# Seven block products for six gate pairs, with weight sums made by accumulating transfers and tiles turned through memory

## The reference

```
h = rms_norm(x); proj = h @ w_in            # 2048 x 24576: q, k, v, z / u, b, c, z / q, k, v, z, three gates
o_a = dilated_mixture_attn(q, k, v) * silu(z)
o_c = b * causal_short_conv(c * u) * silu(z)
o_r = retention(rotary(q), rotary(k), v) * silu(z)
merged = sum over the three mixers of sigmoid(gate) * (o @ w_branch)     # 1536 -> 2048 each
x = x + rms_norm(merged @ w_out)
```

## Time and profile before

| | us |
|---|---|
| median of 3 runs (2746.15 to 2746.77) | 2746.62 |
| span of the profiled execution | 2743.0 |
| PE busy (share of the span) | 2732.6 (100%) |
| DVE busy | 1924.2 (70%) |
| ACT busy | 1222.0 (45%) |
| DMA, queue of SP, share of the 16 engines | 57.4% |

### The profile page before, as it was taken

One profiled execution on the slowest core, in us unless ns is written; L12 is line 12 of the kernel. 1 busy time (PEld: TensorE's weight loads), 2 busy tenths in 40 slices (PEclk: granted clock), 3 DMA queues, 4 the chain that ended last, 5 costly groups with the idle time before them and its releaser, 6 DMA issues.

```text
span 2743.0 us, 30433 instructions
## 1 busy us (share of the span) xinstructions
PE 2732.6 (100%) x12264; PEld 2268.3 (83%) x12264; DVE 1924.2 (70%) x2558; ACT 1222.0 (45%) x1404; POOL 27.5 (1%) x35
## 2 busy tenths in 40 slices
PE   9999999999999999999999999999999999999998
PEld 7888888888888888888878888888888888888887
DVE  6788744777655898858567887457676558977584
ACT  6454544444443334444454545444444433434443
POOL 0000000000000000000000000000000000000000
PEclk9999999999999999999999999999999999999999
DMA  9555566565555555556575555555656565555563
GB/s 333 184 172 196 170 200 194 190 199 188 196 195 190 184 184 176 182 195 221 180 238 175 184 190 179 197 188 187 202 193 198 188 197 177 191 171 182 199 215 138
DMA packets 264732, 529.10 MB, mean 193 GB/s; under 512 B 8464, under 2 KB 8848, under 8 KB 264336
## 3 DMA queue, kind: packets, MB, share of 16 engines
q1 hardware_dynamic: 260976, 517.50, 57.4%
q10 hardware_dynamic: 2608, 4.78, 0.5%
q0 software_dynamic: 1008, 4.87, 0.5%
HBM read 522.94 MB, written 4.19 MB: 192 GB/s over the span
## 4 chain that ended last, share of the span: by engine, by line
PE 99%; DVE 0%; issue 0%; ACT 0%; DVEq 0%; POOL 0%; POOLq 0%
PE ps L651 32%; PE ps L652 32%; PE ps L653 32%; PE ps L586 0%; PE ps L606 0%; PE ps L604 0%; PE ps L603 0%; PE ps L582 0%; PE ps L567 0%; PE ps L587 0%; PE ps L581 0%; PE ps L669 0%; DVE gates L1183 0%; DVE w_trail L913 0%; DVEq L231 0%
## 5 line engine op out<-in xcount | busy, mean ns | idle before, releaser
L913 DVE TENSOR_TENSOR w_trail<-raw,w_lead 128x1024 fp32r<-128x1024 f32 x973 | 1188.7, 1225 | 763.8 <-ACT w_lead L723 754.4
L723 ACT ACTIVATE w_lead<-raw 128x1024 fp32r<-128x1024 f32 x973 | 1028.3, 1060 | 1394.1 <-PE ps L653 1387.3
L651 PE MATMUL ps<-w_lead,hT_lead 128*128 128x512 f32 x3328 | 1299.1, 390 | 0.8 <-issue 0.4
L653 PE MATMUL ps<-w_lead,hT_trail 128*128 128x512 f32 x3328 | 1295.2, 389 | 0.0
L652 PE MATMUL ps<-w_trail,hT_lead 128*128 128x512 f32 x3328 | 1295.1, 389 | 0.0
L651 PEld LDWEIGHTS ps<-w_lead,hT_lead 128*128 128x128 f32 x3328 | 625.0, 188 | 131.1 <-issue 2.2
L653 PEld LDWEIGHTS ps<-w_lead,hT_trail 128*128 128x128 f32 x3328 | 624.9, 188 | 130.0
L652 PEld LDWEIGHTS ps<-w_trail,hT_lead 128*128 128x128 f32 x3328 | 625.1, 188 | 128.4
L651 PE MATMUL ps<-w_lead,oT_lead 128*128 128x512 f32 x576 | 224.3, 389 | 0.0
L653 PE MATMUL ps<-w_lead,oT_trail 128*128 128x512 f32 x576 | 224.1, 389 | 0.0
L652 PE MATMUL ps<-w_trail,oT_lead 128*128 128x512 f32 x576 | 224.1, 389 | 0.0
(11 more groups left out here) (102 smaller groups left out, 781.7 us busy)
## 6 DMA issues: line engine op xcount, KB each, us to landing
raw<-w_in SPq DMA_DIRECT2D x381, 1024.0 KB, 5.1
raw<-w_out SPq DMA_DIRECT2D x32, 1024.0 KB, 5.0
raw<-w_branch_a SPq DMA_DIRECT2D x24, 1024.0 KB, 5.0
raw<-w_branch_c SPq DMA_DIRECT2D x24, 1024.0 KB, 5.0
raw<-w_branch_r SPq DMA_DIRECT2D x24, 1024.0 KB, 5.0
raw<-w_in SPq DMA_DIRECT2D x5, 512.0 KB, 5.0
gates<-x SPq DMA_DIRECT2D x4, 512.0 KB, 13.5
post_gain<-post_norm_g POOLq DMA_DIRECT2D x2, 1024.0 KB, 8.2
```

The costliest lines, as they stand in the source:

```text
L651: pe.matmul(acc, lead[:, k, tok(t)], wl, start=(k == 0), stop=False)
L653: last = pe.matmul(acc, trail[:, k, tok(t)], wl, start=False, stop=(k == BLOCKS[n][2] - 1))
L723: act.activation(w_lead[:, h % SPLIT_SLOTS, :], raw[:, i % RAW_SLOTS, part:part + HALF * COLS], ACT.Copy).then_inc(lead_ready, 1)
L913: dve.tensor_tensor(w_trail[:, s, :], raw[:, i % RAW_SLOTS, part:part + HALF * COLS], w_lead[:, s, :].bitcast(F32), ALU.subtract).then_inc ...
```

## The change

**Seven products.** Gate blocks 2 and 3 of each mixer (three pairs in a layer, six in all) are computed together for contraction tiles 0 to 7. The activations there are four blocks (two token tiles by two chunks), the weights four blocks (two chunks by two gate blocks); eight block products become seven, on sums of blocks. A product takes one chunk and one 128-token operand: two units of 6 matmuls. Contraction tiles 8 to 15 of both blocks stay as they were (eight units of 12). `PAIR_ORDER` gives the order: p1, q3, two plain units, q5, two plain units, p2, p6, p7, two plain, q4, two plain. p1, p6 and p7 accumulate in one side bank, which ACT copies out after each of them; q5 has another.

**Weight sums.** q5, p6 and q4 take the chunk of p1 with a further chunk added to it each time, p7 takes that of q3. POOL issues each addition as a DMA from memory with `accum_op=ADD` into the raw slot, once the chunk's former form has been split: 4 of 1 MB for a pair, 24 in all. The sums of activations are made once a layer, at units 16 to 19 (`form_work` on DVE, `form_lead_of` on ACT).

**Tiles through memory.** q, k, z and the conv product are written to a scratch tensor in memory (512 KB, one DMA on the queue of ACT) and read back as four DMAs of 128 KB that place the 32-row bands; ACT waits for the write before it issues the reads. DVE then turns the tile in 2 instructions of 128x512 in place of 16. For this the evictions write columns in another order, and PE reads the weights of the blocks other than v in runs of 32 columns (`columns`).

**Beside it**: five raw slots, a slot plan (`raw_slots`), the cos and sin tables widened (constants 128x1968 in place of 128x1328), `post_gain` in the v and q tiles, a negated `x_rstd` from POOL.

```diff
-RAW_SLOTS = 4
+RAW_SLOTS = 5
+PAIRED_GATES = {"attention": (2,), "conv": (2,), "retention": (2,)}
+PRODUCTS = {"p1": ((0, 0), None), "q5": ((0, 0), (1, 0)), "p6": ((0, 0), (1, 1)), "p7": ((1, 1), (1, 0)),
+            "q3": ((1, 1), None), "p2": ((0, 1), None), "q4": ((0, 0), (0, 1))}
+PAIR_ORDER = ("p1", "q3", 0, 0, "q5", 0, 0, "p2", "p6", "p7", 1, 1, "q4", 1, 1)
+SUM_AFTER = {"q5": "p1", "p7": "q3", "p6": "q5", "q4": "p6"}
+PAIR_COPY_DUE = {UNIT_AT[kind, n, 1] + AHEAD: (kind, n) for n in PAIRS for kind in ("p1", "p6", "p7")}
+PAIR_REST_DUE = {UNIT_AT[kind, n, 1] + AHEAD + 1: (kind, n) for n in PAIRS for kind in ("p6", "p7")}
+SUM_DUE = {UNIT_AT[before, n, 1]: (kind, n) for n in PAIRS for kind, before in SUM_AFTER.items()}
...
 ACT_DUE = due({
-    "attention": [("exp", 4 * B + 1), ("out", 6 * B + 1)],
+    "attention": [("q_away", 2 * B - 1), ("q_back", 2 * B + 1), ("k_away", 3 * B - 1), ("k_back", 3 * B + 1),
+                  ("exp", 4 * B + 1), ("z_away", 5 * B + 4), ("z_back", 5 * B + 6), ("out", 6 * B + 1)],
...
# SP, a chunk's load
-                    sp.wait_ge(trail_ready, l * HALVES + (2 * i + 2) + (l == 0 and i == RAW_SLOTS))
+                    slot, _before, free_at = SLOT_OF[l, i]
+                    if free_at is not None:
+                        sp.wait_ge(*split_done(*free_at))
...
# POOL
+            def chunk_sum(l, what, n):
+                (i, c), (added, row) = PRODUCTS[what]
+                slot = SLOT_OF[l, CHUNK_LIST.index((n + i, c))][0]
+                wait(*split_done(l, UNIT_AT[SUM_AFTER[what], n, CHUNK // HALF - 1]))
+                pool.dma_start(raw[:, slot, :].rearrange("p (k n) -> p k n", k=CHUNK),
+                               weights[name][:, at:at + CHUNK, col:col + COLS],
+                               accum_op=ALU.add).then_inc(summed[SUMMED_FOR[what]], 16)
...
+                rstd(x_sum, x_mean, l + 1, x_rstd, D_MODEL, 2).then_inc(x_pow, 1)
+                pool.wait_ge(x_pow, l + 1)
+                pool.tensor_scalar(x_neg, x_rstd, -1.0, 0.0, ALU.mult, ALU.add).then_inc(x_rstd_ready, 1)
...
# PE
+            def product(l, h, what, n, part):
+                if part == 0:
+                    if what == "q5":
+                        pe.wait_ge(*side_bank_free(l, q_step))
+                        pe.wait_ge(form_trail, TILES * (l + 1))
+                    elif what in ("p6", "p7"):
+                        pe.wait_ge(pair_copied, 2 * pair_no(l, n) + 1 + (what == "p7"))
+                    elif what == "q3":
+                        pe.wait_ge(*bank_free(l, n + 1))
+                pe.wait_ge(*split_done(l, h))
...
+                for i in range(HALF):
...
+                    pe.matmul(acc[:, :], lead, wl, start=opens, stop=False, skip_group_check=again)
+                    pe.matmul(acc[:, :], lead, wt, start=False, stop=False, skip_group_check=again)
+                    last = pe.matmul(acc[:, :], trail, wl, start=False, stop=closes, skip_group_check=again)
...
+            def columns(n, ap):
+                if kind == "mix" and role != "v":
+                    return ap.rearrange("p (h j a) -> p j h a", h=HPB, j=QUADS)
-                    wl = w_lead[:, slot, i * COLS:(i + 1) * COLS]
+                    wl = columns(n, w_lead[:, slot, i * COLS:(i + 1) * COLS])
...
# ACT
+                elif what in SUM_AFTER and part == 0:
+                    act.wait_ge(*sum_landed(l, what, n))
...
+            def pair_copy(l, what, n):
+                act.wait_ge(*done_product(l, what, n))
+                copied = act.activation(dst, side(l, step)[:, :], ACT.Copy)
...
+            def send_away(l, what, mixer, g):
+                act.dma_start(bounce[to], tile.rearrange("p t c -> p (t c)")).then_inc(away[to], 16)
+            def bring_back(l, what, mixer, g):
+                act.wait_ge(away[to], 16 * trips(l, to, mixer, g))
+                rows = bounce[to].rearrange("(i b) (j c) -> j b i c", i=QUADS, j=QUADS)
+                for j in range(QUADS):
+                    act.dma_start(tile[SQ * j:SQ * (j + 1), :].rearrange("b (i c) -> b i c", i=QUADS),
+                                  rows[j]).then_inc(back[to], 16)
...
+                elif kind == "gate" and n in PAIR_OF:
+                    act.wait_ge(*moved_out(l, n))
+                        act.activation(gates[:, t, cols], gates[:, t, cols], ACT.Sigmoid,
+                                       scale=x_rstd[:, t:t + 1]).then_inc(gate_ready, 1)
...
# DVE
+            def pair_rest_of(l, what, n):
+                rest = dve.tensor_tensor(gates[:, t, COLS * (j + 1):COLS * (j + 2)], side(l, q_step)[:, :],
+                                         gates[:, t, COLS * col:COLS * (col + 1)], ALU.subtract)
...
+            def form_work(l, what):
...
+            def turn_back(l, what, mixer, g):
+                dve.wait_ge(back[to], 16 * QUADS * trips(l, to, mixer, g))
+                for t in range(TILES):
+                    last = dve.transpose(dst[:, :, tok(t)].rearrange("p h (i b) -> p h i b", i=QUADS), squares[:, t])
```

More of the change, by code:

```diff
@@ L75, in layer_blocks @@
                                ("mix", mixer, role, g)))
-        for j in range(OUT_BLOCKS):
-            blocks.append(("w_in", COLS * (GATES_AT + OUT_BLOCKS * b + j), KT, ("gate", mixer, "", j)))
-        for j in range(OUT_BLOCKS):
-            blocks.append((mixer, COLS * j, KT_MIX, ("branch", mixer, "", j)))
+        for kind, j in TAIL[mixer]:
+            if kind == "gate":
+                blocks.append(("w_in", COLS * (GATES_AT + OUT_BLOCKS * b + j), KT, ("gate", mixer, "", j)))
+            else:
+                blocks.append((mixer, COLS * j, KT_MIX, ("branch", mixer, "", j)))
     for j in range(OUT_BLOCKS):
@@ L165, with unit_after @@
 TURNS = ((0, 3), (3, 6), (6, 9), (9, 12), (12, 14), (14, 16))
+STARTS = [0]
+for _kind, _n, _at in UNITS:
+    STARTS.append(STARTS[-1] + (1 if _kind in PRODUCTS else TILES))
+def unit_after(n, at):
+    return next(h for h in range(HALVES) if STARTS[h] >= STARTS[FIRST_HALF[n]] + TILES * at)
 def due(table, offset=0):
@@ new lines @@
+DVE_DUE = due({
+    "attention": [("q", 2 * B + 4), ("k", 3 * B + 4), ("scores", 4 * B), ("sums", 4 * B + 2)]
+                 + pieces("probs", 4 * B + 3) + [("values", 5 * B + 3), ("z", 6 * B), ("out", 6 * B + 2)],
+    "conv": [("prod", 2 * B + 6), ("conv0", 2 * B + 6), ("conv1", 2 * B + 7), ("conv2", 3 * B),
+             ("gate", 4 * B), ("z", 4 * B + 6), ("product", 4 * B + 6), ("out", 4 * B + 7)],
+    "retention": [("q", 2 * B + 6), ("k", 3 * B + 5), ("scores", 3 * B + 7), ("values", 4 * B + 3),
+                  ("norm", 4 * B + 4), ("gate", 4 * B + 5), ("z", 5 * B + 2), ("out", 5 * B + 4)]}, AHEAD)
@@ L215, with side_list @@
 MERGE_TRAIL_DUE = {h + 1: j for h, j in MERGE_LEAD_DUE.items()}
-RESIDUAL_DUE = FIRST_HALF[MERGE_BLOCK0 + OUT_BLOCKS] + AHEAD + 1
+RESIDUAL_DUE = FIRST_HALF[BLOCK_NO["out", "", "", 0]] + AHEAD + 1
+def side_list():
+    steps = [("x", t, j) for t, j in X_ORDER]
+    for h, (kind, n, at) in enumerate(UNITS):
+        if kind in ("p1", "q5") and at == 0:
+            steps.append(("pair", kind, n))
+        for what, mixer, g in PE_DUE.get(h, []):
+            steps += [(what, mixer, g, i) for i in range(HPB if what == "scores" else HPB // 2)]
+        if h in MERGE_DUE:
+            steps += [("merge", MERGE_DUE[h], t) for t in range(TILES)]
+    return steps
+SIDE_LIST = side_list()
+SIDE_STEPS = len(SIDE_LIST)
+STEP = {key: m for m, key in enumerate(SIDE_LIST)}
+READY_STEPS = [sum(key[0] != "pair" for key in SIDE_LIST[:m]) for m in range(SIDE_STEPS + 1)]
+FORMS = {"p6": 0, "q3": 1, "p7": 2, "q5": 3}
+FORM_STEPS = ("whole", "sums", "lead", "trail")
+FORMS_FROM = 2 * B
+PAIR_COPY_DUE = {UNIT_AT[kind, n, 1] + AHEAD: (kind, n) for n in PAIRS for kind in ("p1", "p6", "p7")}
+PAIR_REST_DUE = {UNIT_AT[kind, n, 1] + AHEAD + 1: (kind, n) for n in PAIRS for kind in ("p6", "p7")}
+SUM_DUE = {UNIT_AT[before, n, 1]: (kind, n) for n in PAIRS for kind, before in SUM_AFTER.items()}
+NORM_DUE = {h: g for h, dues in DVE_DUE.items() for what, _mixer, g in dues if what == "norm"}
 def build(nc, x, xT, w_in, w_attention, w_conv, w_retention, w_out, post_g, params, consts, out):
@@ L325, in build @@
         x_mean = sem("x_mean")
+        x_pow = sem("x_pow")
         x_rstd_ready = sem("x_rstd_ready")
@@ L631, in multiply @@
                 kind = BLOCKS[n][3][0]
                 lead, trail = (oT_lead, oT_trail) if kind == "branch" else (hT_lead, hT_trail)
-                slot = h % SPLIT_SLOTS
+                slot = (l * HALVES + h) % SPLIT_SLOTS
+                first = UNITS.index(("half", n, k0)) == FIRST_NORMAL[n]
+                begun = n in PAIR_OF and n != PAIR_OF[n]
                 wait_stationary(l, n, k0, tiles)
-                if k0 == 0 and tiles[0] == 0:
+                if first and not begun and tiles[0] == 0:
```

526 lines of the change are left out of this document (368 added, 158 removed).

## The result

| | before | after |
|---|---|---|
| median, us | 2746.4 (4 runs) | 2851.2 (4 runs, 2849.8 to 2853.2) |
| span of the profiled execution, us | 2743.0 | 2848.1 |
| matmuls of PE | 12264 | 12192 |

The account below looks back on a forecast made before the run. PE was taken as the bound, busy 2732.6 of 2743.0 us. Terms -16.3 + 6.0 + 0.9 + 2.4 + 0.3 = -6.7 gave span 2736.3, with 3.6 to the median 2739.9, said as 2740 us; range 2731 to 2769.

Parts of the forecast that it names:

- Matmuls saved: PE in the gate pairs: 180 matmuls instead of 192 in each of 6 pairs, at 226.7 ns, -16.3 us.
- p7 behind the copy: p6 and p7 share a bank, so PE idles 1.0 us for ACT's copy in each of 6 pairs, +6.0 us.
- q3's bank: q3 waits for ACT to evict gate block 1: 0.05 us late in four pairs, 0.35 in two, +0.9 us.
- Turned tiles: Tiles through memory: DVE is relieved, ACT's added issues and write wait are covered, so 0 us.
- Start of a layer: First v eviction, activation sums and wider tables: PE may miss by a tenth, +0.3 us.
- PE reading in runs of 32: 5184 matmuls reading weights in 16 runs of 128 bytes cost nothing, as strided operands on DVE: 0 us.
- the other end: Alternative estimate for PE's permuted weight reads: +3 to +7 ns a matmul, +16 to +35 us.
- the rival: PE's step grows on the 5184 matmuls: saving gone from 3.1 ns each, 2776 us at 7 ns; chance 0.07.
- Weight sums: POOL's accumulating 1 MB transfers land after 10.0 us, making q4 0.4 us late in 6 pairs, +2.4 us.
- issued at T(4) + 2.52 = 7.96: p6's sum issued 7.96 us after PE starts the pair without stalls, wanted at 19.3, leaving 11.3 us.
- The upper one: Upper bound on a sum's landing, 14.8 us: q5, p6 and q4 3.5, 3.5 and 5.2 us late, 73 us.
- accumulation is processed at half pace: Rival: sums land after 12.5 us, q5, p6 and q4 late, 32 us in all, 2769 us; slow accumulation's chance 0.17.

Follow-up runs that it names:

- the kernel in which nothing of the pairs is late: Changed kernel with permutation in evictions, plain halves behind p6 and p7, addends loaded plainly and added by DVE: 2732.1 us, ratio to before 0.995.
- straight reads with sums: Changed kernel, but PE reads the permuted blocks' weights in straight rows of 512 instead of 16 runs of 32: 2813.3 us.
- the same without: Changed kernel with weights read in straight rows of 512 and the 24 accumulating transfers left out, POOL only signalling: 2736.2 us.
- large scratch: Changed kernel with 8192 bytes of descriptor space for POOL's DMAs instead of 2048, and 4 raw slots instead of 5: 2810.9 us.

## Why the prediction was wrong

- **Matmuls saved, -16.3: right.** 12192 matmuls, and the kernel in which nothing of the pairs is late won 13.6 us, with a pair at 40.8 to 41.1.
- **p7 behind the copy, +6.0: right.** 1.07 less 0.23 us for the gap and 0.11 for the slower step behind it, 0.95 a pair or 5.7 in all (41.78 less 40.83).
- **q3's bank, +0.9: nothing.** No wait of PE at q3 in any run. At the fourth pair, of attention, ACT issued the four reads of z in 1.76 us from 1750.02 on, beside the split that began at 1750.00 and not behind it, and both evictions were done at 1754.87, 2.41 us into the pair and not 2.9.
- **Turned tiles, 0: right,** with the permutation in the evictions 0.5 us from before, inside the interval. DVE's wait for the reads of z, 8.2 us in five places, reaches nobody. DVE fell by 203 us and not 265; without the pairs it fell by 260 (1664.0), and the rest came back with their 36 more splits and additions.
- **Start of a layer, +0.3:** the changed kernel's trace has no such wait; six of the other kernels have one of 0.7 to 0.9 us for the first v eviction. It costs under 1 us.
- **PE reading in runs of 32, 0: wrong, +38.4.** The step inferred PE's price from DVE's rows, where a strided operand costs nothing. I named the other end (3 to 7 ns), and 6.67 ns was in it, but gave the rival 7 in 100 though no row showed PE reading that way. The count was short as well: 5184 left out the u blocks of the convolution, 5760 are permuted. The Trainium skill's rule ("SBUF — State Buffer", section "Door 1: The DMA port swizzle"), by which reads stay fast that hit a 16-byte line twice, would, as I read it, leave all the runs in the table free; for PE the measurements disagree.
- **Weight sums, +2.4: wrong, +77.1** (straight reads with sums, 2813.3, less the same without, 2736.2). The landing was right, 10.0 us against 10.0. What failed is the sentence on p6, "but behind p7's sum, issued at 2.5, in the queue of POOL": I saw the place and still let p6 have 11.3 us, as if the sum ahead of it cost nothing. 40.4 us went because in 2048 bytes POOL issued no second accumulating megabyte before the first had landed (large scratch). By 3 x 10 us, from q5's issue on, p6 had to be some 8 us late (30 less 22.2) by the numbers that stood in the prediction; PE waited 8.3 to 11.3. The remaining 36.7 went by the second half of the same line, "issued at T(4) + 2.52 = 7.96": that is the end of q5's split without a wait, though q5's own sum was let in until 8.4 and takes 10.0. With the large scratch p6's sum was issued 10.2 to 13.6 us into the pair, behind q5's landing and split. Both are prices of the accumulation, since plain loads of the same bytes cost 0.5 us over none: it takes the 16 engines twice as long, and such sums land one after another. Of the 77.1 some 13 are the lower clock behind each long wait, which no term had.

The prediction watched the landing and not the issue. Its bounds stood for a landing, 7.4 to 14.8 us. The upper one was priced at 73 us, near the 77.1, but that nearness is chance: the landings were 8.4 to 11.9, and at 10.0 the forecast had 2.4. The rival "accumulation is processed at half pace" had a part of the mechanism (6.0 against 3.1 us of the engines), and its price, 2769, was wrong, since it took each transfer as slow and not the three as a chain.

## What to carry to other kernels

A transfer that several others precede on one queue is priced as the chain of them, issue to landing, and the time between the first issue and the last need is what must hold it. So is one that may be issued only when the result of an earlier one has been used: take its issue time from that landing, not from the schedule without waits. An accumulating load cost the DMA engines twice a plain one here, in twice the packets, and slowed the loads beside it: where VectorE has over 30% of its time idle, a plain load ahead of time and an addition there are nearly free. A permutation belongs where time is idle: on the evictions it cost nothing here, in the reads of the engine that bounds the kernel it cost 1.4%.
